# Output projection of a fused two-block kernel: attention's rows for both column halves first, then the convolution's rows, token tile by token tile

## The reference

```python
x = layer_norm(x)
attn_l = attend_blocked(...)                       # 8 heads of 64: 512 columns
conv_l = conformer_conv(u_l, ...)                  # silu(layer_norm(dwconv(...))): 512 columns
y_l = concatenate([conv_l, attn_l], axis=-1) @ w_o + b_o
x_mid = layer_norm(ALPHA * x + g1 * y_l, ln1_g, ln1_b)
f_l = conv_ffn(x_mid * (1 + sc2) + sh2, w_up, ...) # 1024 -> 5632, depthwise conv, silu gate -> 1024
x = layer_norm(ALPHA * x_mid + g2 * f_l, ln2_g, ln2_b)
```

## Time and profile before

| | |
|---|---|
| median of 3 runs | 1114.29 us (1113.94, 1114.29, 1117.29) |
| the profiled execution, its own time | 1113.09 us |
| its span, first to last instruction | 1111.3 us |
| outside the span | 1.8 us |
| mean granted TensorE clock | 0.997 |
| TensorE busy | 1085.2 us (98%) |
| DVE busy | 792.6 us (71%) |
| ACT busy | 561.1 us (50%) |
| output projection on TensorE | 688.1 to about 737.9 us of the span |

### The profile page before, as it was taken

One profiled execution on the slowest core, in us unless ns is written; L12 is line 12 of the kernel. 1 busy time (PEld: TensorE's weight loads), 2 busy tenths in 40 slices (PEclk: granted clock), 3 DMA queues, 4 the chain that ended last, 5 costly groups with the idle time before them and its releaser, 6 DMA issues.

```text
span 1111.3 us, 14920 instructions
## 1 busy us (share of the span) xinstructions
PE 1085.2 (98%) x5907; PEld 883.0 (79%) x5907; DVE 792.6 (71%) x1279; ACT 561.1 (50%) x991; POOL 95.2 (9%) x123
## 2 busy tenths in 40 slices
PE   7999999999999999999999999999999999999997
PEld 4678888888888788888867666778888888888886
DVE  5877888888677746758897899786666565545427
ACT  6576666656333447754256675666444444432211
POOL 0221111122322000101000002000000000000001
PEclk9999999999999999999999999999999999999999
DMA  9753433345355753121010211122323232252202
GB/s 379 275 195 115 148 129 117 139 172 199 104 195 223 289 202 114 76 91 56 29 50 1 76 45 69 38 81 109 114 76 114 77 113 88 102 196 89 79 35 76
DMA packets 22368, 135.54 MB, mean 122 GB/s; under 512 B 2545, under 2 KB 2969, under 8 KB 8474
## 3 DMA queue, kind: packets, MB, share of 16 engines
q1 hardware_dynamic: 19936, 128.46, 31.7%
q10 hardware_dynamic: 2362, 6.12, 1.6%
HBM read 132.45 MB, written 2.12 MB: 121 GB/s over the span
## 4 chain that ended last, share of the span: by engine, by line
PE 81%; DVE 8%; ACT 5%; DMA 3%; issue 2%; POOL 1%; SPq 0%; DVEq 0%; ACTq 0%
PE PB L185 79%; DMA RAW<-in_wstream 3%; DVE WL L206 2%; DVE RAW L1455 2%; PE PB L193 2%; ACT WH L199 2%; POOL UPA L206 1%; DVE EARLY L1455 1%; DVE UPA L214 0%; DVE XL L214 0%; SPq L182 0%; ACT DH L199 0%; ACT HH L199 0%; DVE XL L218 0%; DVE AT L234 0%
## 5 line engine op out<-in xcount | busy, mean ns | idle before, releaser
L185 PE MATMUL PB<-HH,WH 128*128 128x512 f32 (+1 forms) x880 | 338.4, 385 | 4.1 <-DVE HL L206 2.0
L206 DVE TENSOR_TENSOR WL<-RAW,WH 128x1024 fp32r<-128x1024 f32 (+3 forms) x172 | 196.6, 1149 | 197.9 <-ACT WH L199 197.4
L185 PE MATMUL PB<-HH,WL 128*128 128x512 f32 (+1 forms) x880 | 332.7, 378 | 0.0
L185 PE MATMUL PB<-HL,WH 128*128 128x512 f32 (+1 forms) x880 | 331.5, 378 | 0.0
L199 ACT ACTIVATE WH<-RAW 128x1024 fp32r<-128x1024 f32 (+3 forms) x172 | 166.6, 975 | 265.6 <-PE PB L185 236.0
L185 PEld LDWEIGHTS PB<-HH,WH 128*128 128x128 f32 x880 | 165.6, 188 | 37.7 <-issue 2.4
L185 PEld LDWEIGHTS PB<-HH,WL 128*128 128x128 f32 x880 | 165.5, 188 | 31.2
L185 PEld LDWEIGHTS PB<-HL,WH 128*128 128x128 f32 x880 | 165.7, 188 | 29.9 <-issue 0.5
L214 DVE SCALAR_TENSOR_TENSOR CV<-VP,PC,CV 128x512 f32<-128x512 f32 x120 | 88.0, 777 | 0.7
L185 PE MATMUL PB<-WL,AH 128*128 128x512 f32 (+1 forms) x198 | 72.4, 366 | 0.0
L185 PE MATMUL PB<-WH,AH 128*128 128x512 f32 (+1 forms) x198 | 72.4, 366 | 0.0
(11 more groups left out here) (299 smaller groups left out, 1707.4 us busy)
## 6 DMA issues: line engine op xcount, KB each, us to landing
RAW<-in_wstream SPq DMA_DIRECT2D x101, 1024.0 KB, 4.9
EARLY<-in_wstream SPq DMA_DIRECT2D x7, 1024.0 KB, 13.9
RAW<-in_wstream SPq DMA_DIRECT2D x5, 768.0 KB, 4.3
RAW<-in_wstream SPq DMA_DIRECT2D x5, 512.0 KB, 3.4
XL<-in_x SPq DMA_DIRECT2D x2, 1024.0 KB, 6.5
HB<-in_x SPq DMA_DIRECT2D x2, 1024.0 KB, 6.3
out<-XL SPq DMA_DIRECT2D x8, 256.0 KB, 2.0
ROWS<-in_rows ACTq DMA_DIRECT2D x3, 512.0 KB, 7.7
```

What stands on the lines that cost most here:

```text
L185: return self.put(lambda e: e.matmul(o, l, r, start=start, stop=stop, skip_group_check=skip))
L206: return self.put(lambda e: e.tensor_tensor(o, a, b, op))
```

## The change

The stream's order is changed, and with it TensorE's. In the new stream, 100 is rows 4, 5 and 101 rows 6, 7 of half 0; 102 is rows 4, 5 and 103 rows 6, 7 of half 1; 104 and 105 are the convolution's rows of half 0, and 106 and 107 those of half 1. TensorE does all of attention's rows for both halves first (the unit of the layer norm's sums stays where it was), then half 0 by token with blocks 104 and 105, then half 1 by token with 106 and 107. The transposes stay ahead of the last unit. `o_residual(i, 0)` now waits for each token tile by itself. The number and the kind of all instructions are unchanged.

```diff
@@ stream_layout
-    for c in (0, 512):
-        rows("w_o_2", (4, c), (6, c))
-        rows("w_o_2", (0, c), (2, c))
+    for r0, r1 in ((4, 6), (0, 2)):
+        for c in (0, 512):
+            rows("w_o_2", (r0, c), (r1, c))
@@ dve_prog
         def o_residual(i, h):
-            tile_done("oy", i, h, B_O + 3, B_O + 7)
+            if i < 3:
+                v.wait_ge(S_.p_sm, ("oy" if h else "oy0", i))
+            else:
+                v.wait_ge(S_.p_blk, B_O + 7 if h else B_O + 5)
@@ pe_prog
-        def second_half(i):
-            ys2[i] = take_aux(("oy", i, 1), i)
-            return rows(ys2, B_O + 4, merged(4), True, False, (i,), False)
-
         rows(ys, B_O, merged(4), True, False)
         conv_sums()
-        for i in (3, 1):
-            second_half(i)
-        rows(ys, B_O + 1, merged(6), False, False)
-        for i in (0, 2):
-            op = second_half(i)
-        op.then_inc(S_.p_blk, B_O + 4)
-        rows(ys, B_O + 2, merged(0), False, False)
-        rows(ys, B_O + 3, merged(2), False, True)
-        by_token(ys2, [(B_O + 5 + n, merged(k)) for n, k in enumerate((6, 0, 2))], "oy",
+        for i in (3, 1, 0, 2):
+            if i == 0:
+                rows(ys, B_O + 1, merged(6), False, False)
+            ys2[i] = take_aux(("oy", i, 1), i)
+            op = rows(ys2, B_O + 2, merged(4), True, False, (i,), False)
+        op.then_inc(S_.p_blk, B_O + 2)
+        rows(ys2, B_O + 3, merged(6), False, False)
+        by_token(ys, [(B_O + 4 + n, merged(k)) for n, k in enumerate((0, 2))], "oy0")
+        by_token(ys2, [(B_O + 6 + n, merged(k)) for n, k in enumerate((0, 2))], "oy",
                  lambda: turn_tiles("h3", 0, XLT, "x2", {0: 0, 1: 1, 2: 2, 3: None}))
```

## The result

The kernel after the change takes 1120.05 us (median of 6 runs, 1118.47 to 1121.66), before it 1114.12 us (median of 6). The ratio is 1.005, with a 95% interval of 1.0036 to 1.0063: slower by 4.0 to 7.0 us. In a second job the same kernel took 1120.16 us (6 runs) against 1113.77, ratio 1.0059 (1.0045 to 1.0073).

The account below looks back on a forecast made before the run. The prediction took TensorE, busy in 98% of the span, as the bound. Its terms, 3.2 + 1.4 + 1.5 = 6.1 us, on an expected median of 1114.3 gave 1120.4 us, range 1117.0 to 1123.0.

Parts of the forecast that it names:

- Term 1: First use of block 105: needed 18 matmuls earlier, before DVE makes its low part; TensorE stalls 3.2 us (2.9 to 3.4).
- Term 2: Transposes: 6 matmuls, not 12, cover DVE's 3.06 us chain from token tile 2; wait grows 1.4 us (1.1 to 1.6).
- Term 3: Mostly behind the block 105 stall: granted clock falls to half for one spell, costing 1.5 us (0 to 1.7).
- The rival without a fall: At the block 105 stall: the clock does not fall, leaving 3.2 + 1.4 = 4.6 us, 1118.9 us; chance 0.25.
- What costs nothing: Output projection: splits of 106 and 107, DVE's three more semaphore waits, the stream and the convolution's row tiles add no time.
- D: At block 105: its low part is ready by 715.1, only the 1.4 us at the transposes stays, 1115.7 us; chance 0.09.
- E: At the transposes and behind: waits of 0.33 and 0.90 us vanish without a stall, at most 1.2 us, 1113.1; chance 0.02.
- C: At the transposes: the clock falls a second time, costing another 1 to 1.5 us, 7.4 in all, 1121.7 us; chance 0.15.

Follow-up runs that it names:

- filled stall: Kernel after the change with block 104's product for token tile 0 added two more times (12 matmuls) ahead of half 0; 1118.22 us, second job 1119.32.
- the first experiment: Kernel after the change with DVE making the low part of block 105 ahead of the four residual rows; 1115.40 us, ratio 1.0013.
- the second experiment: Kernel after the change with half 0 of the convolution's rows done block by block again, 104 on all token tiles, then 105; 1117.94 us.
- early splits: The first experiment with splits of 108 and 109 between half 1's residuals, and tiles 0 and 1 normalized ahead of tile 2's residual; 1119.58 us.
- more cover: The first experiment with both halves of token tile 3 moved last, so 18 matmuls, not 6, stand between token tile 2 and the transposes; 1116.11 us.
- token pairs: As more cover, but each tile in half 0 then half 1; low parts of 105, 106 ahead of the residual rows, 107 behind the first; 1116.71 us.

## Why the prediction was right

The forecast was 1120.4 us, the measurement 1120.05. Terms 1 and 2 came out by their mechanism and nearly by their size. That the whole lies only 0.35 us off is in part luck, since the third term, with bounds of 0 and 1.7 us, is the least certain of all. By its steps:

**Term 1, the stall at block 105 (3.2 us).** The wait is where it was forecast, ended by DVE's low part, 3.04 us long; the third split follows right behind the second and was done by 720.4 on the old scale, as said. The stall's price with the slower restart is 3.23 (filled stall less the first experiment). Moving that one split takes it away. Shown.

**Term 2, less cover for the transposes (1.4 us).** TensorE's time lost there rose from 0.60 to 1.96 us, by 1.36; alone, in the first experiment, it is 1.31 in the stage and 1.4 (0.4 to 2.5) in time. Shown. That the cover is the cause is shown too: with 18 matmuls of it the wait is gone, while DVE's chain is still 3.07 us long.

**Term 3, the clock (1.5 us).** The clock fell at the stall in both profiles after the change, half a microsecond before TensorE went on, and did not in the filled ones. In the profiles it cost 1.3 us with one spell of 3.4 us and 2.9 with 6.8. I had one spell of 3.4: the second profile is that case, and its next stage begins 5.9 us later than before, counted from the sums (forecast: 6), the first one's 7.5. In the medians the size stays open: after the change less filled is 1.8 us in one pair of jobs and 0.8 in the other. The runs' mean clocks speak for about one spell more per run. The rival without a fall (1118.9) is refuted for the profiled executions. It had the Trainium skill behind it, "TensorE: Matmul & The Clock Gate", section on how the clock oscillates, which fears idle gaps longer than this stall; the trace disagrees, with 0.50 granted behind 2.88 us of idle time.

**What costs nothing**: nothing else appeared in the stage; DVE's residuals of half 0 wait 0.75, 2.94, 1.32 and 1.30 us for TensorE and hide their semaphores. The prediction did say that DVE would wait for TensorE there and not be the limit, but not what that is worth. Without going by token in half 0 DVE comes 1.8 us late to token tile 2 (736.38, where the tile ended at 734.58), as the second experiment showed. Term 2 was right only because the change does both.

**Two readings that their rows don't carry.** That an idle time of 1.66 us left the clock full was read from the earlier trace rows. The slices of the earlier trace rows can't show it: the low spell behind 73.33 stands in a 9 too. Windows of 1 us from 22 to 29 have 1.00 throughout, so the statement is true. And the 0.25 us from DVE's low part to the row 738.89 is not in the earlier trace rows; DVE's row is 738.22 with 0.42, so the figure is right.

**The rivals** D and E (the low part in time, a gain) did not occur, and C (a second low spell, at the transposes) did not in the two profiles: the idle times of 1.17 and 0.33 us left the clock at 1.00. C's sum, 7.4 us, is nearly the 7.44 of the first profile, but by another way: there one spell at the stall was twice as long.

## What to carry to other kernels

When an order of matmuls is changed, list for each weight block how many matmuls now stand ahead of its first use, and set that beside the moment when the engine that prepares the block comes to it in its own order: here 18 matmuls fewer turned a margin of 1.1 us into a stall of 3.0. Where a last stretch of work covers another engine's chain, count what is left of it; 6 matmuls of cover fewer cost 1.3 us. And a step put into another engine's gap needs its own input made ahead in time, or the gap becomes a wait (early splits: 4.12 us of idle time on TensorE).

## What the hardware showed unexpectedly

With an idle time of TensorE of 2.88 us or more in the middle of dense work, the granted clock fell to 0.50 in all six profiles that have one (2.88 twice, 2.94, 3.06, 3.65, 4.12). At the idle time of 2.1 us near 73 us of the span, which all twelve profiles have, it fell in seven and not in five: the same wait, with or without a fall. Behind 1.66 us (near 24 us, in all twelve), 1.42, 1.40 and 1.17 it never fell. The fall does not wait for the restart and does not always come with it: by the windows it came 0.6 us ahead of TensorE's going on after the change, 1.0 us behind it with more cover, and 1.7 us behind it near 73 us in the first experiment. A spell lasted 3.4 us or, once, 6.8.

What a spell costs depends on whether TensorE has its work waiting. Behind the stall one of 3.4 us cost 1.3 us. With more cover and with token pairs it lay behind the next stage's first matmul, and from there to the end of the stage it took 20.92 us, against 20.93 before the change. The three small waits that TensorE has there before the change (0.17, 0.45 and 0.46 us) were gone, and the spell cost nothing that can be seen.

Part of the scatter between executions of one kernel comes from such spells. The seven profiles with a fall near 73 us reach the same instruction, a table load of ACT, at 130.1 to 130.5 us, and the five without at 129.0 to 129.3. In the first experiment the five runs with a mean granted clock of 0.999 took 1114.0 to 1114.7 us, and the seven with 0.996 or 0.997 took 1115.3 to 1118.4. All twelve profiles also have the low clock in their last 2 to 5 us, so 0.999 is a run with little else.
